# Eight of sixteen experts per layer computed with the high and low halves of 64 tokens in one stationary tile, and two weight passes in place of three

## The reference, cut to what matters

```python
def routed_moe(x, router_w, router_b, w_gate, w_up, w_down):
    ...
    _, e_idx = lax.top_k(jnp.where(e_mask, sel, -jnp.inf), TOPK_EXPERTS)   # 2 of 16 per token
    w = jnp.take_along_axis(aff, e_idx, axis=1)
    w = w / jnp.sum(w, axis=-1, keepdims=True)
    gates = jnp.einsum('nk,nke->ne', w, jax.nn.one_hot(e_idx, N_EXPERTS, dtype=jnp.float32)).astype(x.dtype)
    y = jnp.zeros_like(xt)
    for e in range(N_EXPERTS):
        h = jax.nn.silu(xt @ w_gate[e]) * (xt @ w_up[e])      # 1024 -> 512, twice
        y = y + gates[:, e:e + 1] * (h @ w_down[e])           # 512 -> 1024
    return y.reshape(B, S, D)
```

## Time and profile before

| | |
|---|---|
| median of 3 runs | 2777.08 us (2775.66 to 2777.76) |
| profiled execution, its own time | 2789.23 us |
| its span | 2787.4 us |
| PE busy | 2514.4 us, 90% of the span |
| DVE busy | 1768.7 us, 63% |
| ACT busy | 1205.5 us, 43% |
| mean granted clock of PE | 0.92 of 2.4 GHz |

### The profile page before, as it was taken

The page is one execution under the profiler, slowest core; times in us unless marked ns, Lnnn a source line. Parts: engine busy times, 40 slices in busy tenths (PEclk is TensorE's granted clock), DMA queues, the critical chain, the costliest instruction groups (busy, mean ns, idle before and its releaser), DMA issues.

```text
span 2787.4 us, 35237 instructions
## 1 busy us (share of the span) xinstructions
PE 2514.4 (90%) x14420; PEld 2168.8 (78%) x14420; DVE 1768.7 (63%) x2174; ACT 1205.5 (43%) x1396; POOL 137.4 (5%) x186
## 2 busy tenths in 40 slices
PE   5898899999778988999799896989989989988997
PEld 5766778887656777888599796769979979566997
DVE  2537557886565755887676668468667667156554
ACT  2424335665344333666443374243334336343432
POOL 4001000000101000000000002000000010210000
PEclk9658999999777999999899998789999999999999
DMA  7303766886201665887488442148858844203551
GB/s 174 121 1 139 249 226 243 298 296 233 106 35 64 233 220 189 294 294 279 157 279 276 165 163 80 61 136 286 273 177 283 273 145 152 91 1 121 182 189 61
DMA packets 241169, 504.74 MB, mean 181 GB/s; under 512 B 10287, under 2 KB 104497, under 8 KB 241008
## 3 DMA queue, kind: packets, MB, share of 16 engines
q1 hardware_dynamic: 216128, 417.84, 43.4%
q10 hardware_dynamic: 21456, 76.89, 7.8%
q0 software_dynamic: 3424, 7.75, 1.2%
HBM read 501.39 MB, written 1.05 MB: 180 GB/s over the span
## 4 chain that ended last, share of the span: by engine, by line
PE 41%; DVE 6%; ACT 2%; issue 1%; ACTq 0%; DVEq 0%
PE PS L916 18%; PE PS L931 9%; PE PS L773 4%; PE PS L733 3%; DVE WGL L1958 1%; PE PS L1307 1%; DVE AR L1961 1%; PE PS L1402 1%; PE PS L953 1%; DVE X L1958 1%; DVE XN L1958 1%; ACT WGH L1490 1%; PE PS L1352 0%; DVE XTL L1958 0%; PE PS L1330 0%
## 5 line engine op out<-in xcount | busy, mean ns | idle before, releaser
L1958 DVE TENSOR_TENSOR WGL<-ring,WGH 128x2048 fp32r<-128x2048 f32 x258 | 589.5, 2288 | 329.0 <-ACT WGH L1490 171.8
L916 PE MATMUL PS<-XTH,WGH 128*128 128x256 f32 x1408 | 403.3, 286 | 7.5 <-DVE XTL L1958 7.4
L916 PE MATMUL PS<-XTL,WGH 128*128 128x256 f32 x1408 | 401.2, 285 | 0.0
L916 PE MATMUL PS<-XTH,WGL 128*128 128x256 f32 x1408 | 401.1, 285 | 0.0
L916 PEld LDWEIGHTS PS<-XTH,WGH 128*128 128x128 f32 x1408 | 272.9, 194 | 13.3 <-issue 9.7
L916 PEld LDWEIGHTS PS<-XTL,WGH 128*128 128x128 f32 x1408 | 272.9, 194 | 4.1 <-issue 1.0
L916 PEld LDWEIGHTS PS<-XTH,WGL 128*128 128x128 f32 x1408 | 272.8, 194 | 0.0
L1958 DVE TENSOR_TENSOR WDL<-ring,WDH 128x1024 fp32r<-128x1024 f32 (+1 forms) x136 | 217.1, 1597 | 77.3 <-ACT WDH L1615 60.7
L1615 ACT ACTIVATE WGH<-ring 128x2048 fp32r<-128x2048 f32 x96 | 184.1, 1917 | 171.2 <-PE PS L981 120.2
L1490 ACT ACTIVATE WGH<-ring 128x2048 fp32r<-128x2048 f32 (+1 forms) x74 | 138.4, 1876 | 195.1 <-PE PS L755 72.0
L1654 ACT ACTIVATE XN<-PS 128x256 f32<-128x256 f32 x88 | 33.9, 385 | 358.4 <-PE PS L916 331.8
(11 more groups left out here) (446 smaller groups left out, 5478.0 us busy)
## 6 DMA issues: line engine op xcount, KB each, us to landing
FA<-in_ada_w ACTq DMA_DIRECT2D x144, 512.0 KB, 6.3
ring<-in_moe_w_up SPq DMA_DIRECT2D x64, 1024.0 KB, 5.6
ring<-in_moe_w_gate SPq DMA_DIRECT2D x64, 1024.0 KB, 7.4
ring<-in_moe_w_down SPq DMA_DIRECT2D x64, 1024.0 KB, 6.2
ring<-in_ffn_w_gate SPq DMA_DIRECT2D x44, 1024.0 KB, 5.5
ring<-in_ffn_w_up SPq DMA_DIRECT2D x44, 1024.0 KB, 9.6
ring<-in_ffn_w_down SPq DMA_DIRECT2D x44, 1024.0 KB, 7.0
ring<-in_hyb_w_in SPq DMA_DIRECT2D x10, 1152.0 KB, 6.6
```

The costliest lines, as they stand in the source:

```text
L916: ins = mm(PS[:, 4 + b, m * T:(m + 1) * T], w_[:, b, w], x_[:, k, :], start=k == 0 and q == 0, stop=k == KD - 1 and q == 2)
L1958: return V.tensor_tensor(out_, x_, y_, op)
```

## The change

The positions 8 to 15 (PACK = 8) are computed for at most 64 picked tokens, in another form:

- `gathered` makes 64 columns in place of 128 (one bank). `picked_high` writes the high part into columns 0 to 63 and `picked_low` the low part into columns 64 to 127 of the same XTH tile.
- `expand_packed` runs this tile against the high and the low weights: two passes per piece of 512 columns in place of three. Rows 0 to 63 of the bank are the high tokens' sums, rows 64 to 127 the low tokens'. ACT copies both banks out (`taken`, 128x512, twice), and `folded` adds the halves and turns them in 8 float32 products with a 128x64 constant (FOLD), in place of the four transposes.
- silu, the product, and the split of the hidden values (`packed_silu`, `packed_hidden`, `packed_high`, `packed_low`) now come after `folded`, on 128x256 in place of 128x512, again with high and low side by side in one tile; `down_picked` makes two passes in place of three.
- The token's gate weight moves from the product to the split of the sums (`sums_high` with a scale, `sums_low` as a scalar-tensor-tensor operation, the latter for all picked positions).
- PE's `marks(i)` stands ahead of the whole down(i-1), not between its halves.
- The side job moves: the products that stood one at each of the positions 5 to 12 stand two at each of 4 to 7, and the third sum moves from position 13 to 8.

```diff
 DENSE = 4
+PACK = 8
-MOD_SLOTS = (2, 4, 13)
+MOD_SLOTS = (2, 4, 8)
 MOD_POINTS = [(1, at) for at in range(6)] + [(2, 0), (2, 1), (2, 4), (2, 5)] + [(3, at) for at in range(6)] + \
-    [(i, 4) for i in range(5, 13)]
+    [(i, at) for i in range(4, 8) for at in (4, 4)]
...
+                def expand_packed(bank, i, h, w):
+                    x0 = (i % 2) * P
+                    for k in range(4):
+                        for m in range(2):
+                            ins = mm(PS[:, bank, :], XTH[:, 4 * h + k, x0:x0 + P], w[m][:, k, :],
+                                     start=h == 0 and k == 0 and m == 0, stop=h == 1 and k == 3 and m == 1)
+                    return ins
+                def folded(i):
+                    pe.wait_ge(S("m_unit"), taken_count(r, i, 1))
+                    for m in range(2):
+                        for c in range(4):
+                            ins = mm(PS[:, 4, (4 * m + c) * 64:(4 * m + c + 1) * 64], UE[:, m, c * P:(c + 1) * P], FOLD,
+                                     start=True, stop=True)
+                    ins.then_inc(S("m_tr"), 1)
...
+                    terms = ((HTH, 0), (HTH, 1), (HTL, 0))[:3 if i < PACK else 2]
...
+                def taken(i, m):
+                    act.wait_ge(S("m_used"), base + PIECE_AT[i, "gate" if m else "up", 1] + 1)
+                    f(UE[:, m, :], PS[:, 5 - m, :], ACT.Copy).then_inc(S("m_unit"), 1)
+                def packed_silu(i):
+                    act.wait_ge(S("m_tr"), units + unit(i) + 1)
+                    f(SGT, PS[:, 4, T:2 * T], ACT.Silu).then_inc(S("m_unit"), 1)
+                def packed_high(i):
+                    act.wait_ge(S("m_h"), units + unit(i) + 1)
+                    f(HTH[:, i % 2, :].rearrange("p (c s) -> p c s", s=P)[:, :, 0:64],
+                      HT.rearrange("p (c s) -> p c s", s=64), ACT.Copy).then_inc(S("m_unit"), 1)
...
+                for i in range(PACK, NE):
+                    after(i, "up", 0)
+                    taken(i, 0)
+                    after(i, "up", 1)
+                    if i < NE - 1:
+                        picked_high(i + 1)
+                    after(i, "gate", 0)
+                    taken(i, 1)
+                    after(i, "gate", 1)
+                    after(i - 1, "down", 0)
+                    sums_high(i - 1)
+                    packed_silu(i)
+                    packed_high(i)
+                    after(i - 1, "down", 1)
...
+                def packed_hidden(i):
+                    dve.wait_ge(S("m_unit"), silu_count(r, i))
+                    tt(HT, SGT, PS[:, 4, 0:T]).then_inc(S("m_h"), 1)
+                for i in range(PACK, NE):
+                    after(i, "up", 0)
+                    after(i, "up", 1)
+                    if i < NE - 1:
+                        picked_low(i + 1)
+                    after(i, "gate", 0)
+                    after(i, "gate", 1)
+                    marks(i)
+                    after(i - 1, "down", 0)
+                    sums_low(i - 1)
+                    packed_hidden(i)
+                    after(i - 1, "down", 1)
+                    packed_low(i)
                     if i + 2 < NE:
                         pick(i + 2)
```

More of the change, by code:

```diff
@@ L124, in constants @@
     c[:, C_SLOT] = p + 0.5
+    c[:, C_IOTA2:C_IOTA2 + P] = p % 64 + 0.5
+    c[:, C_SLOT2] = p % 64 + 0.5
+    c[:, C_FOLD:C_FOLD + 64] = p[:, None] % 64 == np.arange(64)[None, :]
     return c
@@ L1175, in moe @@
                     gate_picked(i)
+                    if i >= PACK:
+                        marks(i)
                     if i > DENSE:
                         down_picked(i - 1, 0)
-                    marks(i)
+                    if i < PACK:
+                        marks(i)
                     if i > DENSE:
                         down_picked(i - 1, 1)
-                    turned(i)
+                    if i < PACK:
+                        turned(i)
+                    else:
+                        folded(i)
                 scattered(NE - 2)
@@ L1696, in picked_high @@
                     act.wait_ge(S("m_xg"), picks + i - DENSE + 1)
+                    if i >= PACK:
+                        f(XTH[:, :, x0:x0 + 64], PS[:, 6, :].rearrange("p (k s) -> p k s", s=64), ACT.Copy)\
+                            .then_inc(S("m_xgh"), 1)
+                        return
                     f(XTH[:, :, x0:x0 + P], PS[:, 6:8, :].rearrange("p b (k s) -> p (b k) s", s=P), ACT.Copy)\
@@ L1704, in sums_high @@
                         act.wait_ge(S("m_sc"), (NE - DENSE - 1) * r.me + i - DENSE)
-                    f(YH[:, :].rearrange("p (b n) -> p b n", b=2), PS[:, 6:8, :], ACT.Copy).then_inc(S("m_yh"), 1)
+                    gate = GS[:, i - DENSE:i - DENSE + 1] if i >= PACK else 1.0
+                    if i >= PACK:
+                        act.wait_ge(S("m_s"), marked(r, i - 1))
+                    f(YH[:, :].rearrange("p (b n) -> p b n", b=2), PS[:, 6:8, :], ACT.Copy, scale=gate)\
+                        .then_inc(S("m_yh"), 1)
+                def taken(i, m):
[8 more added lines that the diff above has]
+                      HT.rearrange("p (c s) -> p c s", s=64), ACT.Copy).then_inc(S("m_unit"), 1)
                 if r.me == 0:
@@ L1753, in moe @@
                 after(DENSE - 1, "down", 1)
-                for i in range(DENSE, NE):
+                for i in range(DENSE, PACK):
                     after(i, "up", 0)
                     after(i, "up", 1)
-                    if i < NE - 1:
-                        picked_high(i + 1)
+                    picked_high(i + 1)
                     after(i, "gate", 0)
@@ L2499, in moe @@
                 marks(DENSE - 1)
-                for i in range(DENSE, NE):
+                for i in range(DENSE, PACK):
                     after(i, "up", 0)
                     after(i, "up", 1)
-                    if i < NE - 1:
-                        picked_low(i + 1)
+                    picked_low(i + 1)
                     after(i, "gate", 0)
@@ L2515, in moe @@
                     products(i, 4)
+                    pick(i + 2)
+                for i in range(PACK, NE):
+                    after(i, "up", 0)
+                    after(i, "up", 1)
+                    if i < NE - 1:
+                        picked_low(i + 1)
+                    after(i, "gate", 0)
+                    after(i, "gate", 1)
+                    marks(i)
+                    after(i - 1, "down", 0)
[3 more added lines that the diff above has]
+                    packed_low(i)
                     if i + 2 < NE:
```

65 lines of the change are left out of this document (48 added, 17 removed).

## The result

The changed kernel takes 2825.28 us (median of 3 runs, 2814.80 to 2826.36) against 2777.08: ratio 1.0163, 95% interval 1.0126 to 1.0201, so slower by 48 us. The forecast was 2792 us, its range ended at 2812. The profiled execution after took 2825.28 us itself (span 2823.5), while that of before stood 12 us above its median; therefore the two spans differ by 36.1 us only.

The account below looks back on a forecast made before the run. PE was taken to bound the kernel before, a 21.8 us loop over ACT and DVE the packed positions after. Forecast: 2777 - 26 (mixtures) + 36 (clock at gathers) + 5 (other clock losses) = 2792 us; range 2748 to 2812.

Parts of the forecast that it names:

- The 21.8 us of the loop over ACT and DVE: Packed positions: the loop of waits through every engine closes after 21.8 us per position, not PE's 18.8.
- its two idle times on DVE: DVE idle about 2.4 us each: behind gate's first half, and at the end for `packed_high` and the high part behind it.
- PE's wait ahead of the gather: In each packed position PE waits 3.0 us for DVE's pick, at 7 gathers per mixture, 14 in all.
- the 18.8 us of PE's own work: PE's work per packed position falls from 22.95 to 18.8 us: 5.6 less in products, 1.4 more for the fold.
- the sign: Whole kernel: slower 0.45, same 0.18, faster 0.37; the forecast turns at a loss of 1.5 us per gather.
- Rivals 1 to 3: Short spells, 2771 to 2783 (0.18); clock mostly holds, 2751 to 2771 (0.25); PE paces at 18.8, about 2710 (with others 0.12).
- Rival 4: Transfers bind: a position's 6.3 MB takes 16.7 us, less than 21.8, so judged hidden; no separate chance given.
- the half clock's loss per gather: Clock loss behind PE's wait ahead of each of 14 gathers: 2.6 us, bounds 0 and 3.7, +36 in all.
- nearer to the long spell: 2.6 us per gather, between spells of 3.3 us (cost 1.65) and 6.3 us (cost 3.2), the latter with low activity behind.
- the row at 1674.93: Profile before: a PE wait of 2.76 us followed by no half clock, taken as evidence that the clock can hold.
- the stretch of positions 5 to 8: Second side-job product ahead of the pick: gathers 7 and 8 late by 0.6 and 1.2 us, 1.8 more; up(9) starts at 23.5.
- the saving at the last position: Last position and end of each mixture: 7.4 us saved in products, 1.4 back for fold, some 1.6 for waits: 4.4 less.

Follow-up runs that it names:

- e5: Changed kernel plus 24 unread fp32r products on PE in place of the wait ahead of each gather of positions 8 to 14: 2778.23 us, ratio 0.9999.
- e3: Changed kernel with DVE's pick ahead of `sums_low` and ACT's last high part ahead of `packed_high`, positions 8 to 15: 2740.50 us, ratio 0.9854.
- e2: Changed kernel with only ACT's last high part of positions 8 to 15 moved ahead of `packed_high`: 2743.36 us, ratio 0.9874.
- e4: Changed kernel with the gather of positions 8 to 15 at 128 columns again, the 64 extra not read: 2785.78 us, ratio 1.0021.
- e9: e3 with the side job back at its old places, one product at each of positions 5 to 12, third sum at 13: 2719.72 us, ratio 0.9797.
- e10: e3 with the pick ahead of the side job's two products at positions 4 to 7 too: 2717.30 us, ratio 0.9782.

## Why the prediction came out as it did

**Right: what takes PE's place.** The 21.8 us of the loop over ACT and DVE, its two idle times on DVE, PE's wait ahead of the gather, and the 18.8 us of PE's own work have all been measured: 21.86 (e5), 2.60 and 2.29 us (e5; about 2.4 predicted for each), 2.70 to 2.78 (3.0 predicted), 18.85 (e3). That `packed_high` in front of the high part causes it is shown by e2, which moves that one line: 19.48 us.

**Right: the sign, and what decides it.** Slower had a chance of 0.45, so this was no safe call. Without the clock's loss the change breaks even (e5: 2778), so the clock decides. Rivals 1 to 3 are out for the kernel as changed: the spells in its loop last 6.8 us and more, the clock held through none of the 14 gathers, and there is no slack in the loop. Rival 4 is out for it too (DMA share 0.69 in a position).

**The step that failed: the half clock's loss per gather was mis-sized.** I took 2.6 us with bounds of 0 and 3.7. Without the clock's loss the six turns would take 20.33 (e4) + 5 x 21.86 = 129.6 us; they take 153.7, so 24.1 / 6 = 4.0 us are lost per gather, above the upper bound. Over 12 turns that is 17 us more than I took, less the 2.4 by which twice six turns are shorter than 6 x 21.8. The reasoning for "nearer to the long spell" pointed the right way; the longest spell that it had was one of 6.3 us, worth 3.2, and behind a wait and in front of 32 passes of 64 columns the spells are 6.8 and 10.2. The upper end of the range was made with 3.7 per gather and still fell short, since it allowed only little for the steps that follow.

The Trainium skill, TensorE: Matmul & The Clock Gate, section "HAM oscillation — how this bites in real kernels", says of a loop whose tiles wait for a transfer for about 3 to 5 us each that every next tile starts cold. The waits here are shorter, 1.17 to 2.78 us, and the trace agrees all the same in 14 of 14 gathers (9 to 15 in both mixtures); in e4, with 128 columns, the clock held behind 5 of the 14. The prediction had weighed that rule against the row at 1674.93.

**Under-priced: the stretch of positions 5 to 8.** It stands 6.1 us above the prediction over both mixtures, for two reasons. The first is a slip in the sum: for position 8 it took `down` at 3.71 us, two passes per piece. But that is down(7), and expert 7 is not packed, so it has 24 products. PE in position 8 after, the first row of down(7) and the fold behind it:

```profile
529.61 0.70 PE L1107 MATMUL PS<-WDH,HTH 128*128 128x512 f32 x2
...
535.17 1.89 PE L1017 MATMUL PS<-XN,XT 128*128 128x64 f32 x16
```

It takes 5.56 us, 1.9 more than in the sum. With the clock at full the stretch takes 72.55 us (e5, second mixture) where the prediction has 71.1 without its terms for the clock: 1.4 us per mixture, 2.9 for both. The slip is more than enough for that, so the lengths of the waits were priced well.

The other 3.2 us are the clock's, and come for the most part from the two side-job products ahead of the pick. I gave 0.6 and 1.2 us for the gathers of 7 and 8, and put the clock's loss only on those from 9 on. DVE in position 6, first mixture:

```profile
461.23 1.28 DVE L2050 SCALAR_TENSOR_TENSOR FA<-FA,ST 128x1024 f32<-128x1024 f32 x1
462.87 1.28 DVE L2050 SCALAR_TENSOR_TENSOR FA<-FA,ST 128x1024 f32<-128x1024 f32 x1 [0.36 <-DMA FA<-in_ada_w]
464.07 0.48 DVE L2044 TENSOR_SCALAR XN<-XN 128x128 f32<-128x128 f32 x2
```

The second product waits 0.36 us for its transfer, which I had "just landing in time", the gather behind is 1.25 us late, the next 1.51, and behind the latter the clock fell for 6.8 us, which I had not priced at all for that gather. In the second mixture that wait was 0.97 us and the clock held, and the stretch is 2.5 us shorter. e9 and e10 show that the waits come from the order on DVE: with it mended the stretch takes 66.9 and 67.5 us instead of 77.6 (e3).

**Over-priced: the saving at the last position.** Predicted 3.4 us net per mixture, measured 1.5; that is 3.7 us over both. e2 and e10 save 5.5 there: the position's own end runs into the same line of ACT's order, which I followed through the loop and not to its last turn, and the wait of 2.24 us that it makes brings another spell of half clock.

The prediction put the counterpart of the profiled execution at 2804 us; it took 2825, 21 more. The three terms give 14.6 + 6.1 + 3.7 = 24.4, and outside the mixtures the program was some 5 us shorter; that leaves 19.7, within 2 us of the 21. The 12 us that the medians lie further apart are those by which the profiled execution of before stood above its median; I had reckoned with the same distance for both, after's has none, and no run explains it.

## What to carry to other kernels

When products are removed from the engine that sets the pace, walk once through the in-order queues of the others: here a loop of 21.86 us stood behind a work of 18.85, in which no engine was the bound, and one line on ACT or on DVE decided it. Put what another engine waits for (the pick) ahead of all that nobody waits for, also in the positions at the edge of the loop. A short wait of PE costs its own length and, in most of the cases here, the half clock behind it; count both, and count the second higher where the work behind the wait is thin.

## What was not expected of the hardware

- The spell at 1.2 GHz behind a wait of 2.7 to 2.8 us depends on the shape of what follows: 6.8 or 10.2 us with passes of 64 columns (after), 3.4 or none with 128 (e4), the passes themselves starting 0.11 us apart in both cases at full clock. Doing twice the columns made the program 39 us faster. Why the long spells alternate between about 6.8 and 10.2 us was not settled.
- Waits of 1.17 and 1.18 us with 64-column passes behind them were enough for the clock to fall in the first turn of both loops; with 128-column passes (e4) the same wait of 1.17 us was not. But waits this short decide nothing by their length: over all runs, of 14 waits of 0.97 to 1.51 us ahead of 64-column gathers the clock fell behind 6 (one of them 0.97 us, e2) and held behind 8 (two of them 1.39 us, e9). What tells the two apart was not settled.
- The 32 passes of 64 columns behind PE work without a gap kept the clock at 1.00 (e5, and e10 with no added work), so 32 thin passes alone do not lower it.
